# Seven products in place of eight for the up projections of two feed-forward blocks

## The reference, cut to what matters

```python
def swiglu(h, w_up, w_down):               # w_up 1024 x 5632, w_down 2816 x 1024
    g, u = jnp.split(h @ w_up, 2, axis=-1)
    return (jax.nn.silu(g) * u) @ w_down

x = x + 0.5 * swiglu(rms_norm(x, g_ffn1[l]), w_ffn1_up[l], w_ffn1_down[l])
h = rms_norm(x, g_mix[l])
...
x = x + mix @ w_out[l]
x = x + 0.5 * swiglu(rms_norm(x, g_ffn2[l]), w_ffn2_up[l], w_ffn2_down[l])
```

## Time and profile before

| | us |
|---|---|
| three runs | 2701.32, 2709.17, 2701.96: median 2701.96 |
| profiled execution, its own time | 2707.99 |
| its span, first to last instruction | 2706.3 |
| second block of layer 0, from PE's end of the output projection to kv's first wait for it | 1010.17 to 1438.55 |
| second block of layer 1 | about 2266 to 2695 |

### The profile page before, as it was taken

The page is one execution under the profiler, slowest core; times in us unless marked ns, Lnnn a source line. Parts: engine busy times, 40 slices in busy tenths (PEclk is TensorE's granted clock), DMA queues, the critical chain, the costliest instruction groups (busy, mean ns, idle before and its releaser), DMA issues.

```text
span 2706.3 us, 44423 instructions
## 1 busy us (share of the span) xinstructions
PE 2585.6 (96%) x18995; PEld 2459.4 (91%) x18995; DVE 1182.1 (44%) x1455; ACT 810.8 (30%) x1019; POOL 101.5 (4%) x205
## 2 busy tenths in 40 slices
PE   6999999999988799999999999999998879999998
PEld 6999999999755599999999999999986559999998
DVE  7333335583354334433454343334543734443343
ACT  5222223443122323222233322222334633222222
POOL 1000000000112100000000100000011020000000
PEclk9999999999889789999999999999997989999999
DMA  5222322222212122223222322322232042223222
GB/s 175 82 85 73 91 80 75 62 67 80 60 56 74 61 63 78 74 82 93 72 68 94 115 78 81 87 80 70 89 121 75 26 146 78 78 69 102 78 60 84
DMA packets 334523, 220.74 MB, mean 82 GB/s; under 512 B 11849, under 2 KB 326497, under 8 KB 334420
## 3 DMA queue, kind: packets, MB, share of 16 engines
q1 hardware_dynamic: 325268, 185.83, 23.8%
q0 software_dynamic: 9152, 33.43, 3.8%
HBM read 206.78 MB, written 12.45 MB: 81 GB/s over the span
## 4 chain that ended last, share of the span: by engine, by line
PE 92%; DVE 5%; ACT 1%; issue 1%; DMA 1%; SPq 0%; POOLq 0%; POOL 0%; DVEq 0%; ACTq 0%
PE psum L519 73%; PE psum L545 6%; PE psum L2156 1%; PE psum L1443 1%; PE psum L1502 1%; PE psum L1494 1%; PE psum L1757 1%; PE psum L1483 1%; PE psum L1740 1%; PE psum L2379 1%; PE psum L1474 0%; PE psum L2202 0%; PE psum L1708 0%; PE psum L2185 0%; DMA x_nat<-in_x_sample 0%
## 5 line engine op out<-in xcount | busy, mean ns | idle before, releaser
L519 PE MATMUL psum<-act_hi,whi 128*128 128x288 f32 (+2 forms) x3504 | 756.1, 298 | 12.4 <-DVE act_lo L786 3.8
L519 PE MATMUL psum<-act_hi,wlo 128*128 128x288 f32 (+2 forms) x3504 | 753.8, 297 | 0.0
L519 PE MATMUL psum<-act_lo,whi 128*128 128x288 f32 (+2 forms) x3504 | 753.1, 297 | 0.0
L519 PEld LDWEIGHTS psum<-act_hi,whi 128*128 128x128 f32 (+2 forms) x3504 | 563.7, 188 | 15.3 <-issue 4.9
L519 PEld LDWEIGHTS psum<-act_lo,whi 128*128 128x128 f32 (+2 forms) x3504 | 564.0, 188 | 0.3
L519 PEld LDWEIGHTS psum<-act_hi,wlo 128*128 128x128 f32 (+2 forms) x3504 | 563.4, 187 | 0.4
L498 DVE TENSOR_TENSOR wlo<-raw,whi 128x2048 fp32r<-128x2048 f32 x190 | 435.4, 2292 | 238.7 <-ACT whi L491 238.5
L491 ACT ACTIVATE whi<-raw 128x2048 fp32r<-128x2048 f32 x190 | 362.0, 1905 | 272.6 <-PE psum L519 268.6
L519 PE MATMUL psum<-h_lo,whi 128*128 128x288 f32 x1408 | 301.9, 295 | 0.0
L519 PE MATMUL psum<-h_hi,wlo 128*128 128x288 f32 x1408 | 301.9, 295 | 0.0
L519 PE MATMUL psum<-h_hi,whi 128*128 128x288 f32 x1408 | 301.9, 295 | 0.0
(11 more groups left out here) (410 smaller groups left out, 2143.2 us busy)
## 6 DMA issues: line engine op xcount, KB each, us to landing
raw<-in_w_ffn_up SPq DMA_DIRECT2D x176, 512.0 KB, 5.0
raw<-in_w_ffn_down SPq DMA_DIRECT2D x64, 384.0 KB, 3.9
raw<-in_w_ffn_down SPq DMA_DIRECT2D x64, 320.0 KB, 3.4
raw<-in_w_out SPq DMA_DIRECT2D x16, 512.0 KB, 4.4
raw<-in_w_in_a SPq DMA_DIRECT2D x14, 512.0 KB, 4.7
raw<-in_w_in_a SPq DMA_DIRECT2D x16, 384.0 KB, 4.0
raw<-in_w_kv SPq DMA_DIRECT2D x12, 512.0 KB, 4.1
vpg<-in_cache_v POOLq DMA_DIRECT2D x16, 384.0 KB, 4.0
```

Of the source, the lines that this page charges most:

```text
L519: last = pe.matmul(psum[0:width, 4 * j + 2 * m + h, 0:HALF], w[:, k, cols], a[:, k, h * HALF:(h + 1) * HALF], start=(k == 0 and step == 0) ...
```

## The change

The two second blocks (`SEVEN_FFN`) get code of their own, written out without loops; the first blocks stay as they are. Their 22 chunks are taken in 11 pairs, in four parts of 3, 3, 3 and 2 pairs, each followed by four down tiles of 256 columns. For a pair, the 1024 features are cut into two halves, giving four weight quarters: A11 and A12 (chunk m, first and last features), A21 and A22 (chunk m+1). The tokens are cut likewise: b11, b12 (first features, first and last 288 tokens), b21, b22 (last features). The plain product of the pair is eight products of a quarter with a token block; the change makes seven:

A11·b11, S1·t1, S2·t2, A12·b21, S3·t3, S4·b22, A22·t4, with S1 = A21+A22, S2 = S1-A11, S3 = A22-S2, S4 = A12-S2, and t1 = b12-b11, t2 = b22-t1, t3 = t2-b11, t4 = b21-t2.

Each product is a "unit": 24 matmuls, a high part by ACT (L1207) and a low part by DVE (L1212) of 128x1024, in one of four slots. `unit_lo` and its high part run three units ahead of PE (`ahead(v)` makes unit v+3). The weight sums are made in place in the raw quarters by DVE (`next_sum`, L1223 to L1231), each right behind a low part, the first when quarters 2 and 3 (A21, A22) have landed. The token sums are made once for each block by GpSimd (`seven_pool`, L1337). The gained tokens x·g are kept in `xg0`, `xg1` (ACT, L1243). A down tile is two units.

The products go back together on DVE: c11 = A11·b11 + A12·b21; u1 = A11·b11 + S2·t2; c21 and c22 from u1, S3·t3 and S1·t1 (three operations); c12 with S4·b22; c21 with A22·t4. ACT first copies A11·b11 and S1·t1 out of PSUM (`keep`, L1445). The scaling by `rinv` is one operation of 1152 elements for both chunks' gates (L1553) and one for both ups (L1526). SP reloads a quarter (512 KB, two DMAs of 256 KB) when the last unit that reads it has its low part, in the order 0, 2, 1, 3; quarter 3 (A22) is read by the last unit. kv's first tile and the end now wait for the last down tile's sum (`down_done`).

```diff
+SEVEN_PARTS = (6, 6, 6, 4)
+SEVEN_FFN = (1, 3)
 ...
+    A11, S1, S2, A12, S3, S4, A22 = range(7)
+    QUARTER = (0, 2, 0, 1, 2, 1, 3)
 ...
+        factors_raw = {"b11": xg0[:, :, first_half], "t1": xg0[:, :, last_half], "t2": xg0[:, :, last_half],
+                       "t3": xg0[:, :, first_half], "b21": xg1[:, :, first_half], "t4": xg1[:, :, first_half],
+                       "b22": xg1[:, :, last_half]}
+        BY_PRODUCT = ("b11", "t1", "t2", "b21", "t3", "b22", "t4")
 ...
+        def unit_lo(dve, W, v):
+            quarter, n = unit_quarter(W, v), unit_columns(W, v)
+            dve.wait_ge(S.part_hi, W.hi(v + 1))
+            dve.tensor_tensor(lo_slots[W.slot[v]][:, 0:n], raw_q[quarter][:, 0:n],
+                              hi_slots[W.slot[v]][:, 0:n].bitcast(F32), ALU.subtract).then_inc(S.part_lo, 1)
+            kind, pair, i = W.units[v]
+            if kind == "up" and i in (W.A11, W.S1, W.S2, W.A12):
+                next_sum(dve, W, pair, i)
+
+        def next_sum(dve, W, pair, i):
+            a11, a12, a21, a22 = raw_q
+            if i == W.A11:
+                for quarter in (2, 3):
+                    dve.wait_ge(S.part_loaded[quarter], W.loads_before(quarter) + W.loaded(quarter, W.pair_at[pair] + W.A22))
+                dve.tensor_tensor(a21, a21, a22, ALU.add).then_inc(S.sums_ready, 1)
+            if i == W.S1:
+                dve.wait_ge(S.sums_ready, W.sums(pair, 1))
+                dve.tensor_tensor(a11, a21, a11, ALU.subtract).then_inc(S.sums_ready, 1)
+            if i == W.S2:
+                dve.wait_ge(S.sums_ready, W.sums(pair, 2))
+                dve.tensor_tensor(a21, a22, a11, ALU.subtract).then_inc(S.sums_ready, 1)
+            if i == W.A12:
+                dve.tensor_tensor(a12, a12, a11, ALU.subtract).then_inc(S.sums_ready, 1)
 ...
+                    unit_hi(act, W, 0, base)
+                    unit_hi(act, W, 1, base)
                     act.wait_ge(S.tile_done, n + 1)
-                    gained_hi(act, 0, gains)
-                    gained_hi(act, 1, gains)
+                    for k in range(QD):
+                        act.activation(act_hi[:, k, first_half], xg0[:, k, first_half], ACT.Copy).then_inc(S.b_hi, 1)
+                    act.wait_ge(S.t_ready, W.t(1))
+                    factor_hi(act, W, "t1")
 ...
+                    x_gained(2 * t + m)
+                    unit_hi(act, W, 2, base)
 ...
+                    unit_lo(dve, W, 0)
+                    unit_lo(dve, W, 1)
+                    first_lo(0)
+                    first_lo(1)
 ...
+                    first_lo(2)
+                    first_lo(3)
+                    factor_lo(dve, W, "t1")
+                    unit_lo(dve, W, 2)
 ...
+                for pair in W.pairs_of[part]:
+                    m = 2 * pair
+                    for quarter in (0, 2, 1, 3):
+                        if pair == 0:
+                            sp.wait_ge(S.lo_ready, base + 3 + quarter // 2)
+                        else:
+                            v = W.pair_at[pair - 1]
+                            sp.wait_ge(S.part_lo, W.lo(v + {0: W.A12, 2: W.S3, 1: W.S4, 3: W.A22}[quarter] + 1))
+                            if quarter == 0:
+                                sp.wait_ge(S.sums_ready, W.sums(pair - 1, 4))
+                        load_up(pair, m + quarter // 2, quarter)
 ...
+            def factor(out, a, b):
+                pool.tensor_tensor(out, a, b, ALU.subtract).then_inc(S.t_ready, 1)
+            pool.wait_ge(S.xg_ready, W.xg(QD))
+            factor(factors_raw["t1"], factors_raw["t1"], factors_raw["b11"])
+            pool.wait_ge(S.xg_ready, W.xg(KD))
+            pool.wait_ge(S.b_lo, W.factor("t1"))
+            factor(factors_raw["t2"], factors_raw["b22"], factors_raw["t1"])
+            pool.wait_ge(S.t_ready, W.t(2))
+            factor(factors_raw["t3"], factors_raw["t2"], factors_raw["b11"])
+            pool.wait_ge(S.b_lo, W.factor("b21"))
+            factor(factors_raw["t4"], factors_raw["b21"], factors_raw["t2"])
 ...
+            def up_unit(v, ready=None):
+                pe.wait_ge(S.part_lo, W.lo(v + 1))
+                elif ready:
+                    pe.wait_ge(S.b_lo, W.factor(name))
+                for s, k in order:
+                    if ready == "by chunk" and s == 0:
+                        pe.wait_ge(S.b_lo, W.factor("b11") - QD + k + 1)
+                    for step, (w, a) in enumerate(((hi, factors_hi), (hi, factors_lo), (lo, factors_hi))):
+                        last = pe.matmul(psum[:, bank + s, 0:HALF], w[:, k, s, :], a[name][:, k, :],
+                                         start=(k == 0 and step == 0), stop=(k == QD - 1 and step == 2))
+                last.then_inc(S.part_done, 1)
 ...
+                    if p == 0 and part:
+                        pe.wait_ge(S.down_done, W.down(4 * part - 1))
+                    elif pair == 1:
+                        pe.wait_ge(S.rinv_kept, norm + 1)
+                    elif p:
+                        pe.wait_ge(S.c_step, W.c(pair - 1, 2))
+                    up_unit(v + W.A11, "by chunk" if new else None)
+                    if p:
+                        pe.wait_ge(S.c_step, W.c(pair - 1, 3))
+                    up_unit(v + W.S1, new)
+                    if p:
+                        pe.wait_ge(S.c_step, W.c(pair - 1, 6))
+                    elif part:
+                        pe.wait_ge(S.down_done, W.down(4 * part))
+                    up_unit(v + W.S2, new)
 ...
+                    else:
+                        ahead(v)
+                        if left is not None:
+                            h_high(left[0], 0, left[1])
+                            silu(left[0], 1)
+                        ahead(v + 1)
+                        keep(v + W.A11, 0)
+                        if left is not None:
+                            h_high(left[0], 1, left[1])
+                        ahead(v + 2)
+                        keep(v + W.S1, 1)
+                        for i in range(3, 7):
+                            ahead(v + i)
+                    silu(ups, 0)
+                    left = (ups, 2 * p)
 ...
+            def ahead(v):
+                if v + 3 < W.n:
+                    unit_lo(dve, W, v + 3)
 ...
+            def u1(pair):
+                dve.wait_ge(S.part_done, W.done(W.pair_at[pair] + W.S2 + 1))
+                dve.wait_ge(S.p_copied, W.copied(pair, 1))
+                dve.tensor_tensor(mixed[:, 0, :, last_half], p_kept[0], both(up_bank(W, pair, W.S2)), ALU.add).then_inc(S.c_step, 1)
 ...
+            def c22(pair):
+                dve.wait_ge(S.part_done, W.done(W.pair_at[pair] + W.S3 + 1))
+                dve.wait_ge(S.c_step, W.c(pair, 1))
+                dve.tensor_tensor(mixed[:, 1, :, first_half], mixed[:, 0, :, last_half], both(up_bank(W, pair, W.S3)),
+                                  ALU.add).then_inc(S.c_step, 1)
+                dve.wait_ge(S.p_copied, W.copied(pair, 2))
+                dve.wait_ge(S.c_step, W.c(pair, 3))
+                dve.tensor_tensor(mixed[:, 1, :, last_half], mixed[:, 1, :, first_half], p_kept[1], ALU.add).then_inc(S.c_step, 1)
+                dve.tensor_tensor(mixed[:, 0, :, last_half], mixed[:, 0, :, last_half], p_kept[1], ALU.add).then_inc(S.c_step, 1)
 ...
+                    else:
+                        ahead(v)
+                        if left is not None:
+                            h_low(left[0], 0, left[1])
+                            mix(left[0], 1)
+                        ahead(v + 1)
+                        if left is not None:
+                            h_low(left[0], 1, left[1])
+                        ahead(v + 2)
+                        u1(pair)
+                        ahead(v + 3)
+                        c11(pair)
+                        ahead(v + 4)
+                        c22(pair)
+                        ahead(v + 5)
+                        c12(pair)
+                        ahead(v + 6)
+                    mix(ups, 0)
+                    left = (ups, 2 * p)
 ...
-                    pe.wait_ge(S.region_free0, N_TILES // 2)
-                    pe.wait_ge(S.region_free1, N_TILES // 2)
+                    pe.wait_ge(S.down_done, sevens[1].down(16))
 ...
         def kv_pe(pe, nth, norm):
+            pe.wait_ge(S.down_done, sevens[0].down(16))
```

More of the change, by code:

```diff
@@ L61 @@
 BASE_FFN.append(BASE_OUTB + 4)
[L62 removed]
+N_TILES = BASE_FFN[3]
 class Count:
@@ new lines, in build, with up_bank @@
+        BY_PRODUCT = ("b11", "t1", "t2", "b21", "t3", "b22", "t4")
+        p_kept = [tmp[x].rearrange("p (s n) -> p s n", s=2) for x in range(2)]
+        FIRST_BANKS = (0, 2, 4, 0, 2, 4, 0, 6, 2, 4, 0)
+        def up_bank(W, pair, i):
+            part = next(x for x, pairs in enumerate(W.pairs_of) if pair in pairs)
+            at = 7 * (pair - W.pairs_of[part][0]) + i
+            if part == 0:
+                return FIRST_BANKS[at if at < 7 else 7 + (at - 7) % 4]
+            return 2 * ((at + 2 * (part % 2)) % 4)
```

(38 more changed lines are left out.)

404 lines of the change are left out of this document (366 added, 38 removed).

## The result

The changed kernel takes 2692.49 us (median of 20 runs, 2678.17 to 2698.74), the kernel before 2706.86 (20 runs, 2692.36 to 2712.48): a ratio of 0.995, 95% interval 0.9937 to 0.9963, so 13.5 us faster, between 10 and 17. Forecast were 28 (2674 against 2701.96, a median of three runs; twenty give 2706.86, so the gains are compared here and not the times). The direction was right and half of the gain is missing.

The account below looks back on a forecast made before the run. PE, busy 96% of the span, was taken to bound the kernel. 70.4 - 20.6 - 16.4 - 1.9 - 0.6 - 3 = 27.9 us faster: 2674 against a median of 2701.96, range 2654 to 2708.

Parts of the forecast that it names:

- What PE loses: In both blocks, 168 matmuls a pair in place of 192: 528 fewer at 0.1333 us, 70.4 us.
- DVE's price: DVE's work in a pair: 1.14 us for each 1024-element operation, 22.9 us in all against 22.4 on PE.
- rival B: DVE pays full busy times: each pair's loop 1.6 us longer, 27 of 28 us given back, 2701; chance 12%.
- The reload loop: Inside the parts, the next pair's first sum waits for quarter 3's reload: 25.0 us a pair in saturated stretches.
- L = 3.9: Time in us from A22's low part until quarter 3's 512 KB reload is there; bounds 3.3 to 5.7.
- The stalls: PE's waits inside the parts and at their first down tiles: 10.3 us a block, 20.6 in both.
- Rival D: Slower: quarter 3 comes later, behind another quarter in the queue; 2727 at a reload time of 6.5 us; chance 12%.
- The start: At each block's beginning, first product at about 6.8 us, waits for t2 and t3; 16.4 us given back in two blocks.
- GpSimd: At the block's start, a token subtraction of 1152 elements takes 2.7 us, between 1.15 and 3.5.
- rival C: GpSimd and DVE exclude each other, so t2 and t3 come later; 13 us in all, 2687; chance 23%.
- Clock: Longer PE idles at the start bring half clock again: 3 us for both blocks, bounds 0 and 8.
- kv's edge: After the block, kv waits for a sum of 1152 elements before its first chunks: 1.9 us.

Follow-up runs that it names:

- little of quarter 1: Changed kernel with three quarters of quarter 1's reload left out, so later pairs compute with old weights there; one run, 2677.59 us.
- The run on the token sums: Changed kernel with the four token subtractions made by VectorE instead of GpSimd; ratio to the kernel before 0.9914 (0.9883 to 0.9946).
- the one with GpSimd in mid-block: Changed kernel plus a memset and six GpSimd subtractions in each block's fifth pair, on memory nobody else uses; one run, 2715.61 us.
- the run on kv's edge: Changed kernel with kv waiting for 15 of 16 down tiles and its first weights' low part behind the last but one sum; one run, 2686.23 us.

## Why the prediction was half right

- **What PE loses**: right. 528 matmuls fewer.
- **DVE's price**: right. 1024-element operations start 1.13 to 1.14 us apart at 1.22 busy, and without the reload's wait a pair takes 23.1 to 23.5. So rival B is out. The Trainium skill's sentence behind it (VectorE: DVE Perf Modes, "The DRAIN you can't avoid"), that the next operation waits until the pipe is empty, does not hold for these rows; the same paragraph limits it, as a next operation "that is not held starts earlier", and the prediction left that out.
- **The reload loop: the step that failed, by a mis-sized term.** "I take L = 3.9" was read from a transfer with an empty queue. In the saturated pairs quarter 3 stands behind quarter 1, and L is 4.6 to 5.2, the loop 25.7 to 26.3 and not 25.0. The mechanism (third pairs late, down tiles making it up) is as described; part 2 lost 4.4 us to it where 1.8 were forecast. The stalls, forecast at 20.6 for both blocks, came to 29.6: what the blocks gave back (428.3 - 418.7 and 428.3 - 418.2 off 35.2 each, 25.6 and 25.1) less 21.1 for the start. That is 9 of the 13 us that are missing. The stalls for an L of 3.9 were themselves put too high: with little of quarter 1 (L 3.8 to 4.6, second pairs at 39.2 and 39.5) the same sum gives 13.9, so the two errors in this term partly cancel. Rival D named the mechanism, a quarter behind another in the queue; it came part of the way to the 5.8 from which it would have decided.
- **The start: right in sum, by two errors that cancel.** 16.4 and some 3 for the clock were forecast, 21.1 measured (second pairs at 38.2 and 39.5 where 31.5 was, and 3.2 of products each). The prediction took the low part at 1002.03 for the one that frees buffer 1 ahead of the block. It is that of the block's own first tile; the one that matters ended at 991.5. Behind it SP issued the loads into buffer 1, before (the first two of the four in its row) and now (quarters 2, 1 and 3):

```profile
989.23 2.29 DVE L498 TENSOR_TENSOR wlo<-raw,whi 128x2048 fp32r<-128x2048 f32 x1 [0.76 <-ACT whi L491]
```

```profile
991.70 13.79 SPq L908 DMA_DIRECT2D raw<-in_w_ffn_up  x4
```

```profile
991.64 3.38 SPq L1303 DMA_DIRECT2D raw<-in_w_ffn_up  x6
```

  So the first product came at 1.1 and not at 6.8. Against that, S2 waited 6.8 us and not 2.3. That the sum came out near is luck.
- **GpSimd**: the price was right, 2.69 us a subtraction for the 2.7 taken. That they shut DVE out was rival C, with the loser the other way round: it is DVE's list that came late, by 2.2 to 2.5 us three times. The run on the token sums and the one with GpSimd in mid-block show it. The trace agrees with the Trainium skill's lock (SBUF — State Buffer, "Who interferes with whom"), also in that PSUM inputs and a memset do not meet it.
- **Clock**: as feared for the start, the granted clock was half (third last column) from 1020.9 to 1027.7; PE stood idle from 1016.0 to 1022.83. S2's 24 matmuls took 5.61 and 5.35 us in the two blocks in place of 3.2, 4.6 us together where 3 were taken; the 21.1 above include them.

```profile
1020.90:1027.70 6.80, 4.87 (x20) 4.90 (x21) 6.80 (x5) 3.15 (x5) 3.56 (x1) 0.50 0.00 0
```

- **kv's edge**: forecast 1.9, measured 4.6 (1010.17 to 1449.65 gave 439.5; 1007.75 to 1442.31 now gives 434.6, 4.9 less where the block is 9.6 shorter). Of the 4.6, 2.0 went in the run on kv's edge; there the low part of kv's first weights no longer stands ahead of the last sum on DVE, as it does here:

```profile
1425.93 2.29 DVE L610 TENSOR_TENSOR wlo<-raw,whi 128x2048 fp32r<-128x2048 f32 x1 [0.74 <-ACT whi L603]
1428.26 1.36 DVE L1618 SCALAR_TENSOR_TENSOR x_t<-psum,x_t 128x1152 f32<-128x1152 f32 x1
```

  and kv's first products then ran at half clock (0.50 from 1430.5 to 1433.9). The end's 0.6 was right (0.5).

Given back in all: 29.6 + 21.1 + 4.6 + 0.5 = 55.8 of 70.4, where 42.5 were forecast; 14.6 us remain, as the runs say.

## What to carry to other kernels

When a change takes work from the engine that sets the pace, the next thing to set it is not the next engine's busy time but its loop with what it waits for: here a buffer freed by the last user and wanted by the first. Price such a reload with the transfers that stand ahead of it in that very place, and if the loop is closer than a few per cent to the pace, break it with a second buffer before tuning anything else: 4 KB a partition that lay idle were worth more than the whole change. And check which iteration a row in the trace belongs to by the row that it releases, before a sum is built on it.

## What the hardware showed that was not expected

VectorE and GpSimd take turns: beside six subtractions of 1152 elements one behind the other on GpSimd (17.65 us), VectorE got through six operations with both inputs in the core's memory; those of 1024 elements start 3.05 us apart (1172.80, 1175.85) in place of 1.14. So a subtraction that GpSimd takes over, 1.3 us on VectorE, costs VectorE 1.9 to 2.5 in return where it meets such an operation. And a restart is dear: behind 6.8 us without work 24 matmuls took 5.61 us in place of 3.2, at half the granted clock.
